# A two-layer hybrid decoder step on one core: sample tokens first between the two layers, loads in smaller pieces

## The reference, cut to what matters

```
x = LN(a*x + mixer(x))
x = LN(a*x + moe(x))                          # 16 experts, two per token
x = x + sigmoid(x @ Wg + bg) * (p @ Wp)       # "the gate"
```

```
q, k, v, qi, ki, wi = split(x @ w_in)         # 1024+256+256+512+64+8 columns
q, k, qi, ki = rope(q), rope(k), rope(qi), rope(ki)
score[q, key] = sum over 8 heads of wi * relu(qi . ki)     # over past and new keys
idx = top_k(score)                            # 256 of 1088 keys for sample rows, 64 of 256 for prompt rows
```

## Time and profile before

| | us |
|---|---|
| median of 3 runs | 1497.34 (1495.82 to 1498.2) |
| the profiled execution: its own time | 1494.89 |
| its span, first to last instruction | 1493.1 |
| PE busy | 1257.4 (84%) |
| DVE busy | 501.7 (34%) |
| ACT busy | 340.4 (23%) |
| POOL busy | 42.3 (3%) |

### The profile page before, as it was taken

One profiled execution on the slowest core, in us unless ns is written; L12 is line 12 of the kernel. 1 busy time (PEld: TensorE's weight loads), 2 busy tenths in 40 slices (PEclk: granted clock), 3 DMA queues, 4 the chain that ended last, 5 costly groups with the idle time before them and its releaser, 6 DMA issues.

```text
span 1493.1 us, 21283 instructions
## 1 busy us (share of the span) xinstructions
PE 1257.4 (84%) x7455; PEld 642.1 (43%) x7456; DVE 501.7 (34%) x1101; ACT 340.4 (23%) x741; POOL 42.3 (3%) x70
## 2 busy tenths in 40 slices
PE   6998888897969999888699870599896999989865
PEld 3445666665533333333344540366643333323322
DVE  1013445445341111111640369744434111111163
ACT  1113333334012121111111140255501212211110
POOL 1100000000100000001000100000010000000100
PEclk9999999998979999999899995699997999999978
DMA  9764877856539899997721344135423989999721
GB/s 336 308 225 170 329 264 309 330 230 225 180 127 373 333 382 401 404 403 296 272 80 30 89 117 120 49 106 177 140 93 132 382 329 389 401 405 401 294 91 36
DMA packets 146735, 364.29 MB, mean 244 GB/s; under 512 B 17856, under 2 KB 34272, under 8 KB 141296
## 3 DMA queue, kind: packets, MB, share of 16 engines
q1 hardware_dynamic: 137664, 328.79, 59.3%
q0 software_dynamic: 6320, 25.78, 5.1%
q10 hardware_dynamic: 2688, 8.91, 1.6%
HBM read 341.48 MB, written 21.97 MB: 243 GB/s over the span
## 4 chain that ended last, share of the span: by engine, by line
PE 66%; DMA 14%; DVE 12%; issue 3%; ACT 2%; POOL 0%; SPq 0%; DVEq 0%; ACTq 0%; POOLq 0%
PE PS L568 12%; DMA ring<-in_moe_w_up 12%; PE PS L840 11%; PE PS L967 5%; PE PS L861 5%; PE PS L753 5%; PE PS L784 4%; PE PS L650 3%; PE PS L703 2%; PE PS L692 2%; PE PS L663 2%; DVE PR L1986 2%; DVE PR L1984 2%; PE PS L603 2%; PE PS L1156 1%
## 5 line engine op out<-in xcount | busy, mean ns | idle before, releaser
L840 PE MATMUL PS<-ring,QKV 128*64 128x512 f32 (+1 forms) x512 | 228.2, 594 | 25.0 <-DMA ring<-in_moe_w_up 21.2
L843 PE MATMUL PS<-ring,QKV 128*64 128x512 f32 (+1 forms) x512 | 228.1, 594 | 0.0
L568 PE MATMUL PS<-ring,XT 128*128 128x512 f32 (+3 forms) x704 | 183.5, 472 | 11.3 <-DMA ring<-in_a_w_in 8.6
L1187 ACT ACTIVATE QKV<-PS 128x512 f32<-128x512 f32 (+5 forms) x180 | 94.8, 527 | 372.1 <-PE PS L568 158.5
L840 PEld LDWEIGHTS PS<-ring,QKV 128*64 128x64 f32 (+1 forms) x512 | 70.2, 140 | 171.5 <-issue 146.1
L568 PEld LDWEIGHTS PS<-ring,XT 128*64 128x64 f32 (+1 forms) x704 | 87.7, 165 | 105.6 <-issue 92.2
L861 PE MATMUL PS<-ring,QKV 128*64 128x512 f32 (+1 forms) x512 | 123.8, 598 | 0.2
L784 PE MATMUL PS<-X,QKV 128*64 128x512 f32 x432 | 103.1, 613 | 3.1 <-DVE QKV L1784 3.1
L1793 DVE TENSOR_TENSOR QKV<-QKV,PS 64x512 f32<-64x512 f32 (+1 forms) x32 | 21.8, 680 | 232.6 <-ACT QKV L1337 232.6
L1187 ACT ACTIVATE KP<-PS 128x512 f32<-128x512 f32 (+1 forms) x112 | 64.5, 580 | 115.5 <-PE PS L650 83.3
L1187 ACT ACTIVATE XT<-PS 128x512 f32<-128x512 f32 (+4 forms) x136 | 55.3, 442 | 131.9 <-PE PS L547 93.4
(11 more groups left out here) (289 smaller groups left out, 1353.2 us busy)
## 6 DMA issues: line engine op xcount, KB each, us to landing
ring<-in_moe_w_gate SPq DMA_DIRECT2D x32, 2048.0 KB, 13.9
ring<-in_moe_w_up SPq DMA_DIRECT2D x32, 2048.0 KB, 18.6
ring<-in_moe_w_down SPq DMA_DIRECT2D x32, 2048.0 KB, 16.6
ring<-in_cache_a_k SPq DMA_DIRECT2D x64, 512.0 KB, 6.9
ring<-in_cache_a_v SPq DMA_DIRECT2D x64, 512.0 KB, 7.6
ring<-in_a_w_in SPq DMA_DIRECT2D x6, 2048.0 KB, 20.8
places<-OR POOLq DMA_DIRECT2D x8, 1024.0 KB, 15.2
ring<-in_ple_gate_w SPq DMA_DIRECT2D x4, 2048.0 KB, 14.1
```

The costliest lines, as they stand in the source:

```text
L568: ins = pe.matmul(PS[p0:p1, banks[u % 4], 0:c1 - c0], XT[:, k, t0:t0 + rows], wt[:, k, c0:c1], start=(k == 0), stop=(k == KD - 1))
L840: ins = pe.matmul(PS[0:m, 0, :], XE[:, k, 0:m], wg[:, k, :], start=(k == 0), stop=(k == KD - 1))
L843: ins = pe.matmul(PS[p1:p1 + m, 1, :], XE[:, k, 0:m], wu[:, k, :], start=(k == 0), stop=(k == KD - 1))
L1187: ins = act.activation(dst, src, ACT.Copy) if scale is None else \
```

## The change

- **Start:** the first weight piece is loaded as four quarters of two chunks each, and PE does that piece chunk by chunk over all three tiles (`project_first`). POOL loads the constants, the page table and the small parameters only after the last quarter has landed.
- **Experts:** gate and up weights are loaded as halves (gate, up, gate, up); the halves of a slot are given free one by one, as `experts_used` now counts at chunk 0, chunk 4 and the next rows.
- **Between the layers:** after layer 0 the tiles go in the order sample, prompt 0, prompt 1; after layer 1 as before. Norm and gate go by tile, with both column halves together: DVE gates the first tile before it adds up the third. In layer 0 the sample tile's projection is done between the gates. The second half of the gate weights is loaded once the first tile's expert results have been gathered, not after its norm.
- **Layer 1's input:** the projection's units have a new order, sample units first; the sample tile's index scores and sums stand between them. The sort follows at once, ahead of the prompt selection, which now comes after the merge. Prompt index scores stand between the last units. PE turns the sorted lists after the last unit, after two key transposes and after the prompt keys.
- **GpSimd** rotates all but the sample's indexer part, doubles keys, clears buffers and adds up the prompt index scores, which ACT now weights; half of the kidx pages are loaded from its queue. kidx has no ring slot any more. Buffers of the index work lie in the slot of a small projection piece, whose next load waits for the selection.
- **Stores of y** go tile by tile.

In the diff, names that only change (semaphores) are left out:

```diff
+GATE_ORDER = ((2, 0, 1), (0, 1, 2))
+
+B_WIDTH = (512, 512, 512, 512, 72)
+B_UNITS = ((3, 2), (4, 2), (2, 2), (0, 2), (1, 2), (4, 0), (3, 0), (4, 1), (3, 1),
+           (2, 0), (0, 0), (1, 0), (2, 1), (0, 1), (1, 1))
+B_BANK = (4, 7) + (5, 4) * 7
...
                   .then_inc(S(f"x_landed{t}"), 16)
-            for j in range(6):
+            for q in range(KD // 2):
+                sp.dma_start(ring[:, 0, 1024 * q:1024 * q + 1024].rearrange("p (k n) -> p k n", k=2),
+                             a_w_in[0].rearrange("(p k) n -> p k n", k=KD)[:, 2 * q:2 * q + 2, 0:512])\
+                  .then_inc(S(f"a_in_first_landed{q}"), 16)
+            for j in range(1, 6):
...
+                def gate_up_half(e, j, half):
...
+                    w = (moe_w_gate, moe_w_up)[j % 3]
+                    sp.dma_start(ring[:, s, 2048 * half:2048 * half + 2048].rearrange("p (k n) -> p k n", k=4),
+                                 w[layer, bass.ds(e, 1)].rearrange("a (k p) n -> p (a k) n", p=P)[:, 4 * half:4 * half + 4])\
+                      .then_inc(landed[s], 16)
+
+                def expert(e, first, free):
+                    for half in range(2):
+                        for j in range(first, first + 2):
+                            free(j, half)
+                            gate_up_half(e, j, half)
+                    free(first + 2, 0)
+                    s = (n0 + first + 2) % SLOTS
+                    sp.dma_start(ring[:, s, :], moe_w_down[layer, bass.ds(e, 1)].rearrange("a (p k) n -> (a p) (k n)", p=P))\
+                      .then_inc(landed[s], 16)
...
+                    for first in (0, 3):
+                        def free(j, half):
+                            used = EXPERT_USED[2] if j % 3 == 2 else 2 + half
+                            if j % 3 != 1:
+                                sp.wait_ge(*at(f"experts_used{layer}", i * 6 + (first - 6 + used)))
+
+                        expert(i * 2 + first // 3, first, free)
...
-                sp.wait_ge(*at(f"normed{layer}1", 1))
+                sp.wait_ge(*at(f"tile{GATE_ORDER[layer][0]}_moved{layer}", 32))
                 columns(("ple_g", layer, 1), ple_gate_w[layer], 512, 1024, True)
...
+                    for j in (3, 4, 2):
+                        columns(("b_in", j), b_w_in[0], 512 * j, 512 * j + B_WIDTH[j], True)
+                    for r in range(2):
+                        kx = KX[r].rearrange("p (j b d) -> p j b d", j=NPAGE, b=2)
+                        for bb in range(2):
+                            for j in range(NPAGE):
+                                pg = page_id(2 * r + bb, j)
+                                sp.dma_start(kx[:, j, bb, :], cache_b_kidx[0, bass.ds(pg, 1)].rearrange("a p d -> (a p) d"))\
+                                  .then_inc(k_landed[r], 16)
+                    for j in (0, 1):
+                        columns(("b_in", j), b_w_in[0], 512 * j, 512 * j + B_WIDTH[j], True)
...
+            pool.wait_ge(*at(f"a_in_first_landed{KD // 2 - 1}", 16))
...
+            def prompt_index(t):
+                rotate(t, OFF_QI, HI + 1, 16, "cosI", "sinI")
+                pool.tensor_scalar(WI[:, t, :], QKV[:, t, OFF_WI:B_IN], IDX_SCALE, None, ALU.mult)
+                ki = QKV[:, t, OFF_KI:OFF_WI].unsqueeze(1).to_broadcast([P, 2, HD])
+                link(pool.tensor_copy(QKV[:, t, DUP_I:DUP_I + 128].rearrange("p (u d) -> p u d", u=2), ki))
+                pool.sem_inc(S("index_doubled"), 1)
+                store_index_keys(t)
+
+            def add_index_scores(u):
+                m, t = u // 2, u % 2
+                kw = 128 * (t + 1)
+                pool.wait_ge(*at("pi_weighted", u + 1))
+                for c in range(2):
+                    acc = PB[:, t, 0:kw]
+                    begin = causal[:, t, 0:kw] if m == 0 and c == 0 else acc
+                    link(pool.tensor_tensor(acc, SM[:, u % 2, 256 * c:256 * c + kw], begin, ALU.add))
+                pool.sem_inc(S("pi_added"), 1)
+
+            def keys_and_queries(t):
+                rotate(t, 0, HB + KVB, 8, "cosA", "sinA")
+                if t < 2:
+                    k = QKV[:, t, OFF_K:OFF_V].rearrange("p (g d) -> p g d", g=KVB)
+                    dk = QKV[:, t, DUP_K:DUP_K + 512].rearrange("p (g u d) -> p g u d", g=KVB, u=2)
+                    pool.tensor_copy(dk[:, :, 0, :], k)
+                    link(pool.tensor_copy(dk[:, :, 1, :], k))
+                pool.sem_inc(S("rotated1"), 1)
+                store_keys(t)
+
+            def b_input():
+                for r in range(2, 4):
+                    kx = KX[r].rearrange("p (j b d) -> p j b d", j=NPAGE, b=2)
+                    for bb in range(2):
+                        for j in range(NPAGE):
+                            pg = pool.value_load(pt_sb[0:1, bass.ds((2 * r + bb) * NPAGE + j, 1)], min_val=0,
+                                                 max_val=pool_pages - 1)
+                            pool.dma_start(kx[:, j, bb, :], cache_b_kidx[0, bass.ds(pg, 1)].rearrange("a p d -> (a p) d"))\
+                                .then_inc(S("kidx_landed"), 16)
+                pool.wait_ge(*at("kidx_mm", 4))
+                pool.memset(QBB, 0.0).then_inc(S("qb_zero"), 1)
+                pool.wait_ge(*at("qkv_evac1", 5))
+                keys_and_queries(2)
+                pool.wait_ge(*at("sample_rotated", 1))
+                store_index_keys(2)
+                pool.wait_ge(*at("kidx_mm", 8))
+                pool.memset(OR[:, 0:NK], 0.0).then_inc(S("or_zero"), 1)
+                pool.wait_ge(*at("sis_mm", 9))
+                pool.memset(QZI, 0.0).then_inc(S("pi_zero"), 1)
+                for t in range(2):
+                    pool.wait_ge(*at("qkv_evac1", 7 + 2 * t))
+                    prompt_index(t)
+                for u in range(4):
+                    add_index_scores(u)
+                pool.wait_ge(*at("qkv_evac1", 12))
+                keys_and_queries(0)
+                for u in range(4, 8):
+                    add_index_scores(u)
+                pool.wait_ge(*at("qkv_evac1", 15))
+                keys_and_queries(1)
+                pool.memset(QZ, 0.0).then_inc(S("pq1_zero"), 1)
...
+            def project_first():
+
+                w = ring[:, 0, :].rearrange("p (k n) -> p k n", k=KD)
+                for k in range(KD):
+                    if k % 2 == 0:
+                        pe.wait_ge(*at(f"a_in_first_landed{k // 2}", 16))
+                    for t, (t0, rows) in enumerate(TILES):
+                        for p0, p1, c0, c1 in pieces(t, 512):
+                            ins = pe.matmul(PS[p0:p1, 4 + t, 0:c1 - c0], XT[:, k, t0:t0 + rows], w[:, k, c0:c1],
+                                            start=(k == 0), stop=(k == KD - 1))
+                        if k == KD - 1:
+                            ins.then_inc(S("qkv_mm0"), 1)
...
-                        if k == 0:
+                        if k in (0, 4):
                             ins.then_inc(S(f"experts_used{layer}"), 1)
...
+                gate_turn(layer, 0)
+                gate_mm(layer, 0, 0)
+                gate_mm(layer, 0, 1)
+                gate_turn(layer, 1)
+                gate_mm(layer, 1, 0)
+                if layer == 0:
+                    token_turn(0, (7, 4))
+                gate_mm(layer, 1, 1)
+                if layer == 0:
+                    pe.wait_ge(*at("token_turn_evac", 1))
+                gate_turn(layer, 2)
+                if layer == 0:
+                    unit(0)
+                    unit(1)
+                gate_mm(layer, 2, 0)
+                if layer == 0:
+                    token_turn(1, (4, 7))
+                    sample_index_turn()
+                gate_mm(layer, 2, 1)
...
+            def unit(n):
+
+                j, t = B_UNITS[n]
+                t0, rows = TILES[t]
...
+            new_scores()
+            kidx_turn(0)
+            unit(2)
+            new_sum()
+            kidx_scores(0)
+            kidx_turn(1)
+            unit(3)
+            kidx_sum(0)
+            kidx_scores(1)
+            kidx_turn(2)
+            unit(4)
+            kidx_sum(1)
+            kidx_scores(2)
+            kidx_turn(3)
+            token_turn(2, (4, 5))
+            kidx_sum(2)
+            kidx_scores(3)
+            unit(5)
+            sample_turn()
+            kidx_sum(3)
+            for n in range(6, 10):
+                unit(n)
+            prompt_keys_turn()
+            pe.wait_ge(*at("kidx_evac", 8))
+            for m in range(2):
+                query_chunk("pi", m, OFF_QI + m * 128)
+            for n in range(10, 14):
+                unit(n)
+                for u in range(2 * (n - 10), 2 * (n - 10) + 2):
+                    prompt_index_scores(u)
+            unit(14)
...
+            pe.wait_ge(*at("rotated1", 3))
+            for t in range(2):
+                for g in range(KVB):
+                    ins = pe.transpose(PS[:, t, g * 128:g * 128 + 128],
```

(67 more changed lines are left out.)

766 lines of the change are left out of this document (403 added, 363 removed).

## The result

The changed kernel takes 1415.47 us (median of 4 runs, 1414.03 to 1418.84) against 1496.58 us (4 runs): a ratio of 0.9457, 95% interval 0.9436 to 0.9478, some 81 us less. 1423 was forecast, 1412 to 1434 for the forecast's own case. The profiled execution took 1416.22 us with a span of 1414.5, 78.6 less than the span before.

| landmark (start or end, us) | before | after | ahead by | gained in the stage |
|---|---|---|---|---|
| first product of layer 0's projection | 19.59 | 11.87 | 7.7 | 7.7 |
| first product after the projection | 127.68 | 121.48 | 6.2 | -1.5 |
| first gate product of layer 0's experts | 440.46 | 434.37 | 6.1 | -0.1 |
| last down product of layer 0 ends | 698.77 | 691.03 | 7.7 | 1.6 |
| first gathered tile is added, layer 0 | 710.42 | 701.50 | 8.9 | 1.2 |

The account below looks back on a forecast made before the run. PE was taken to bound most of the span, except DVE's sort and the weight loads late in each expert stage. 8 + 4 + 55.5 + 7 = 74.5; 1494.9 - 74.5 + 2.45 = 1423 us, range 1398 to 1450.

Parts of the forecast that it names:

- the forecast's own case: Whole kernel: the summed terms hold, giving 1423 us, range 1412 to 1434, chance 0.55.
- Start: Layer 0's projection: first product at about 11.6 instead of 19.59, as quarters land sooner; -8 us, bounds 0 and -8.2.
- Experts: Expert stages: half loads fill one gap, the rest of the lead being lost at the long expert; -2 us per layer.
- Rival 1: Expert stages give back their whole shortage, loads running ahead through the long expert: 1411, at most 1399; chance 0.20.
- Gates and sample units: Layer 0's gates and first sample units: 52.6 us of PE work, ending at 771; no gain, but 4.5 us of projection done.
- Sort and what follows: Layer 1's input: sort hidden beside PE, then rotation, turns, merge and selection; attention at 901.5 against 957, -55.5 us.
- Rivals 2 and 3: POOL late at three waits: 1435 to 1450, chance 0.13; sample-score interleaving stalls, sort outlasting unit 14: 1448, chance 0.08.
- Sparse attention: Layer 1's attention: page loads start later, but PE asks for each about 10 us after it lands; 0 us.
- Tail: After layer 1's experts: earlier first gate turn, evacuation at once, one small last store; -7 us, bounds 0 and -10.
- Rival 4: Expert stages: halves load at a lower rate, +92 us per layer, about 1610 (1517 by the skill's page); chance 0.04.
- the 2.45 added for the median: Whole time: the earlier kernel's median of 1497.34 lay 2.45 us above its profiled execution, so this was added at the end.

Follow-up runs that it names:

- the quarters' run: Changed kernel with expert gate and up weights loaded in quarters of 0.5 MB, a quarter slot freed after every second chunk: 1416.92 us, ratio 0.9475.
- select_first: Changed kernel with DVE doing the prompt selection before the merge of the sorted halves instead of behind it: 1414.53 us, ratio 0.9458.

## Why the prediction was right, and where it was not

- **Start** (-8; 7.7 at the first product, 6.2 at the end of the projection). The size is nearly right by luck, as two steps were wrong. The first is that the quarters alone bring the first data in by 11.4, at "1.3 us apart at 402 GB/s": with GpSimd's loads beside them the first products start at 15.99, not 11.87. The hold on these loads, which I counted only as a wait that is covered, brings 5.0 us at the second piece, the quarters 1.4. The second is "an eighth of a 17.5 us piece is 2.2 us": chunk by chunk it is 2.50, so the first piece costs 2.5 us more (20.0 for 17.5). The net loss there is only 1.5 (21.9 against 20.5, from 19.59 to the last evacuation at 40.12), as the slow first products cost 1.9 us now and 3.0 before: the first few are 0.85 us apart in both traces, later ones 0.43. An estimate from these rows: one load with the hold, done tile by tile, would begin the second piece at 13.65 + 20.5 = 34.2, only 0.4 later than quarters chunk by chunk. That was not run.
- **Experts** (-2 per layer; -1.6 and -1.9). Right, by the step that said the lead is lost at the long expert: whole loads put 1.9 back, and without the long expert the halves are worth 3.6. The half that was to fill the gap is issued 3.6 us after the long expert's down load (512.40, 508.81); a whole piece came 7.0 after it before. Rival 1 falls; in the quarters' run not even finer pieces recover the shortage.
- **Gates and sample units.** The forecast's times behind the first add are held here against the trace less 8.9, the lead at that point. The first turn of a gate came at 709.57, where 718.5 - 8.9 = 709.6 was forecast. The gates and the first two sample units ended at 758.5 for 771 - 8.9 = 762.1: 48.9 us for the 52.6 of the sum.
- **Sort and what follows** (-55.5; -58.9). Right in mechanism, with some terms off. The sample's scores took 30.6 us (758.5 to 789.1, PE busy throughout) for the 31.4 forecast: the products cost 2 us more than 28.4, but none of the 3 us for round trips through ACT showed. The nine units and the prompt's index work took 66.5 for 63.4, 1.5 of it a wait for DVE's copies. So unit 14 ended at 855.6 for 857.1. The sort ends 11 us before that, so it is off the path, as forecast. From unit 14 to the merge it took 9.6 us for 11.5: GpSimd's rotation needed 3.8 us, not 4.5, the transposes and turns 5.1 for 5.5 (867 + 4.5 + 2.5 + 3 is 877.0, where the prediction writes 877.5). Rivals 2 and 3 fall by the same rows.
- **Sparse attention** (0; -1.2). Nothing was lost, but "PE asks for each about 10 us after it lands" was too generous at the end. It fits the third pair's keys (issued until 930.45, asked for at 942.36). The last pair's are issued until 965.65 and asked for at 972.27; in select_first such a load had landed 1.6 us after its last issue, so some 5 us of slack are left, an estimate. select_first shows what comes of it: when attention starts 12.9 us earlier with the mask no sooner, 10.5 us are lost, 6.0 of them in waits for pages.
- **Tail** (-7; -7.0). 3.4 us of it are the second tile's sums. From the last gate's end to the end of the span it takes 11.6 us (1402.93 to 1414.5) for 11.9 before (1481.24 to 1493.1), so the single small store brings some 0.3. The rest, the evacuation that no longer stands behind three roots and the gates by tile, was not taken apart.
- **Rival 4** falls by the late windows: 403 GB/s with halves, 403 with quarters, 402 with whole pieces. The Trainium skill (DMA: Bandwidth & Descriptors, Measured) gives 78% of peak for a load of 1 MB, measured there on loads issued from GpSimd. These loads are issued from SyncE with several in flight; no run here shows such a loss, and the measurement decides.
- **GpSimd.** Its rotation's five steps took 2.97 us for 960 elements a partition, the longest, of 128x320, 0.90 us against DVE's 0.49. The Trainium skill (GPSIMD Engine Reference, 3.1 Elementwise) gives about twice DVE's time; the trace agrees.

Left out of the sum were 1.2 us between experts and norm, where the sample's 64 rows are now gathered first, and 1.2 us in attention; neither was tested. Of the 7.5 us between 1423 and the median, 4.2 lie in the stages (1494.9 - 74.5 = 1420.4 against the profiled 1416.22). The rest is the 2.45 added for the median, which here lies 0.75 under the profiled execution.

## What to carry to other kernels

A long serial step on one engine costs nothing once enough work for another engine, which does not need its result, is put beside it (the sort's 52.8 us here); after that, look at what the next engine has queued ahead of the hand-over, here a turn that waited for a rotation it did not need (some 15 us). Ask of each reordering which loads the moved step sets free: 12.9 us on DVE were worth 2.4 with the mask late, 15.4 were worth 15.3 with the mask early. And finer pieces help only as far as the ring's next full stop: look for the one slot that comes free last.
